# Delta rule: its inputs loaded in front of the cache copies, and the copies made in 4 KB rows, keys and values apart

## What is computed

```python
cache = caches[gi]                       # (8, min(win, 1024), 2, 8, 128): rows of keys and values
L = cache.shape[1]
kv_new = jnp.stack([k[:, :, gi], v[:, :, gi]], axis=2)
kv_all = jnp.concatenate([cache, kv_new], axis=1)
keep = min(win, L + T)                   # T = 4
bufs.append(kv_all[:, L + T - keep:])    # returned as the new cache
```

```python
vnew = ui - wi @ S
o = (qi * exp(gi)) @ S + ai @ vnew
S = S * exp(glast) + (ki * exp(glast - gi)).T @ vnew
```

## Time and profile before

| what | value |
|---|---|
| median of 3 runs | 2547.58 us (2545.9 to 2551.32) |
| the profiled execution | 2549.36 us, of it 2547.6 us in the span |
| TensorE busy | 2061.0 us, 81% of the span |
| VectorE busy | 1281.7 us, 50% |
| ScalarE busy | 778.5 us, 31% |
| GpSimd busy | 645.0 us, 25% |
| DMA | 874.97 MB moved, mean 343 GB/s |
| norm phase | 8.6 to 21.2 us |
| input projection | 21.2 to 117.7 us |
| convolution phase | 117.7 to 239.1 us |
| delta phase | 239.1 to 462.2 us |

### The profile page before, as it was taken

One profiled execution on the slowest core, in us unless ns is written; L12 is line 12 of the kernel. 1 busy time (PEld: TensorE's weight loads), 2 busy tenths in 40 slices (PEclk: granted clock), 3 DMA queues, 4 the chain that ended last, 5 costly groups with the idle time before them and its releaser, 6 DMA issues. The chain is left out here.

```text
span 2547.6 us, 25620 instructions
## 1 busy us (share of the span) xinstructions
PE 2061.0 (81%) x9026; PEld 1031.3 (40%) x9026; DVE 1281.7 (50%) x3157; ACT 778.5 (31%) x2275; POOL 645.0 (25%) x645
## 2 busy tenths in 40 slices
PE   7893797478787898877699999987888887988766
PEld 5682685243222243322244464554532222432222
DVE  0084643264677667775511031123556677666754
ACT  1141100024444344443411122121234444344443
POOL 0000000034443444434201000000344434454341
PEclk9985766789999999998799999999899999999978
DMA  5894999679999999999938755753899999999995
GB/s 196 306 339 137 335 331 332 236 268 405 427 427 427 427 427 414 427 426 427 411 147 335 276 200 206 284 199 125 338 426 426 427 427 427 426 423 427 427 427 243
DMA packets 129427, 874.97 MB, mean 343 GB/s; under 512 B 15876, under 2 KB 29700, under 8 KB 45195
## 3 DMA queue, kind: packets, MB, share of 16 engines
q0 software_dynamic: 92160, 662.74, 62.6%
q1 hardware_dynamic: 37139, 210.60, 23.4%
HBM read 861.98 MB, written 118.81 MB: 385 GB/s over the span
## 5 line engine op out<-in xcount | busy, mean ns | idle before, releaser
L1430 PE MATMUL tail_acc<-tail_ring,tail_diag 128*128 128x512 f32 x1216 | 597.7, 622 | 111.5 <-ACT tail_diag L1289 110.6
L1177 DVE CUSTOM_DVE_ANT_0 tail_ring<-tail_ring,all_h 128x1024 f32<-128x1024 f32 x344 | 418.8, 1223 | 235.8 <-DMA tail_ring<-in_peer_uv,tail_idx 235.3
L1430 PE MATMUL tail_acc<-mid_wring,tail_diag 128*128 128x512 f32 x832 | 413.3, 624 | 98.7 <-ACT tail_diag L1289 98.5
L1570 POOL DMA_INDIRECT mid_wring<-in_peer_uv,tail_idx x232 | 239.0, 1030 | 1001.7 <-DVE all_x L1062 525.8
L1570 POOL DMA_INDIRECT tail_ring<-in_peer_uv,tail_idx x344 | 369.4, 1074 | 480.4 <-PE tail_acc L1430 410.8
L1430 PEld LDWEIGHTS tail_acc<-tail_ring,tail_diag 128*128 128x128 f32 x1216 | 217.0, 193 | 477.2 <-ACT tail_diag L1289 297.3
L1177 DVE CUSTOM_DVE_ANT_0 mid_wring<-mid_wring,all_h 128x1024 f32<-128x1024 f32 x232 | 283.3, 1223 | 175.4 <-DMA mid_wring<-in_peer_uv,tail_idx 174.1
L1283 ACT ACTIVATE tail_gelus<-tail_dots 128x1 f32<-128x1 f32 x576 | 116.2, 202 | 723.3 <-DVE tail_dots L1177 723.0
L1430 PEld LDWEIGHTS tail_acc<-mid_wring,tail_diag 128*128 128x128 f32 x832 | 147.8, 193 | 352.6 <-ACT tail_diag L1289 223.9
L1681 PE MATMUL mix_acc<-mid_wring,all_hT 128*128 128x512 f32 x576 | 273.4, 610 | 1.5 <-PEq L80 1.4
L1289 ACT ACTIVATE tail_diag<-all_ident,tail_weights 128x128 f32<-128x128 f32 x512 | 205.5, 401 | 26.4 <-PE tail_acc L1430 9.9
(11 more groups left out here) (363 smaller groups left out, 2099.3 us busy)
## 6 DMA issues: line engine op xcount, KB each, us to landing
mid_wring<-in_w_qkv SPq DMA_DIRECT2D x18, 2048.0 KB, 8.8
out_kv_s<-in_cache_kv_w SPq DMA_DIRECT2D x8, 4064.0 KB, 49.2
mix_ring<-in_kT POOLq DMA_DIRECT2D x16, 1024.0 KB, 8.1
mix_ring<-in_v_rows POOLq DMA_DIRECT2D x16, 1024.0 KB, 10.3
ab_ring_w<-in_w_in_ab SPq DMA_DIRECT2D x6, 2048.0 KB, 11.4
mix_ring<-in_kT POOLq DMA_DIRECT2D x16, 768.0 KB, 9.3
mix_ring<-in_v_rows POOLq DMA_DIRECT2D x16, 768.0 KB, 9.0
mid_wring<-in_w_out SPq DMA_DIRECT2D x4, 2048.0 KB, 10.4
```

The costliest lines, as they stand in the source:

```text
L1177: V.tensor_tensor_reduce(out=u, in0=u, in1=h[:, g, :], scale=1.0, scalar=0.0, op0=ALU.mult, op1=ALU.add, accum_out=dots[:, n:n + 1]).then_ ...
L1430: last = mm(acc[g][:, c * 512:(c + 1) * 512], diag[:, n % DIAGS, :], v[:, c * 512:(c + 1) * 512], start=first, stop=final)
L1570: pool.indirect_dma_start(slot(r), None, table, bass.IndirectOffsetOnAxis(ap=idx[:, j, i:i + 1], axis=0)).then_inc(landed[r], 16)
```

## The change

The allocation of the delta phase's loaded tiles and the list of their 14 loads move into a new function, `delta_inputs`, called in front of the norm phase; the tiles live from there to the end of the delta phase. `first_norm_phase` gets the list as `later` and SP issues it right behind the three chunks of weights. `delta_phase` takes the tiles and the semaphore. In `roll_cache` every copy becomes two, one of the keys and one of the values, each of `keep` rows of 1024 words (4 KB) that lie 8 KB apart on both sides; the last wait counts twice as many.

```diff
--- before.py
+++ after.py
@@ -147,7 +147,7 @@
 
 
-def first_norm_phase(nc, K, T, hT, ahead):
+def first_norm_phase(nc, K, T, hT, ahead, later):
 
     x, xs, h, hs = K["x"], K["xs"], K["h"], K["hs"]
     with ExitStack() as ctx:
@@ -166,6 +166,8 @@
                 sp.dma_start(gain[:], broadcast_rows(T["norm_mix"][0:1, :], D)).then_inc(gain_in, 16)
                 sp.dma_start(gain_s[:], T["gain_s"][0]).then_inc(gain_in, 16)
                 for to, frm, landed in ahead:
+                    sp.dma_start(to, frm).then_inc(landed, 16)
+                for to, frm, landed in later:
                     sp.dma_start(to, frm).then_inc(landed, 16)
 
             @block.vector
@@ -566,7 +568,22 @@
 
 
-def delta_phase(nc, name, K, T, hT, zT, conv, mixT, cache_out):
+def delta_inputs(P, T):
+
+    G = {"cst": P.sb("masks", [128, 12, 128]), "own": P.sb("owner", [128, DEC_B]), "wab": P.sb("w_ab", [128, KC, 8]),
+         "alog": P.sb("a_log", [128, 4]), "dtb": P.sb("dt_bias", [128, 4]), "gn": P.sb("norm_gain", [128, 1]),
+         "S0": P.sb("S_sample", [128, DEC_B, 4, 128])}
+    loaded = P.sem("delta_loaded")
+    loads = [(G["wab"][:], T["w_in_ab"][0].rearrange("(k p) n -> p k n", p=128)[:, :, IN_AB - 8:IN_AB], loaded),
+             (G["cst"][:], T["c_gdn"].rearrange("p (k n) -> p k n", k=12), loaded),
+             (G["own"][:], T["c_owner"], loaded), (G["alog"][:], broadcast_rows(T["a_log"], 4), loaded),
+             (G["dtb"][:], broadcast_rows(T["dt_bias"], 4), loaded),
+             (G["gn"][:], T["gdn_norm_g"].rearrange("a n -> n a"), loaded)]
+    loads += [(G["S0"][:, b, :, :], T["state_delta"][0, b].rearrange("h k v -> k h v"), loaded) for b in range(DEC_B)]
+    return G, loaded, loads
+
+
+def delta_phase(nc, name, K, T, G, loaded, hT, zT, conv, mixT, cache_out):
 
 
@@ -601,10 +618,7 @@
 
     with ExitStack() as ctx:
         P = Phase(nc, ctx, name)
-        cst = P.sb("masks", [128, 12, 128])
-        own = P.sb("owner", [128, DEC_B])
-        wab = P.sb("w_ab", [128, KC, 8])
-        alog, dtb, gn = P.sb("a_log", [128, 4]), P.sb("dt_bias", [128, 4]), P.sb("norm_gain", [128, 1])
+        cst, own, wab, alog, dtb, gn, S0 = (G[k] for k in ("cst", "own", "wab", "alog", "dtb", "gn", "S0"))
         ab, gt = P.sb("ab", [128, 3, 8]), P.sb("g_tmp", [128, 3, 4])
         beta, g = P.sb("beta", [128, 3, 4]), P.sb("g", [128, 3, 4])
         per_tile = lambda name, shape: [P.sb(f"{name}{t}", shape) for t in range(3)]
@@ -618,12 +632,11 @@
         Rv, Rk, kd = per_tile("Rv", [128, 4, 128]), per_tile("Rk", [128, 4, 128]), P.sb("k_decay", [128, 3, 4, 128])
         u, wT, qe = P.sb("u", [128, 3, 4, 128]), P.sb("wT", [128, 3, 4, 128]), P.sb("q_exp", [128, 3, 4, 128])
         S, vn, vs = P.sb("S", [128, 4, 128]), P.sb("v_new", [128, 4, 128]), P.sb("v_new_s", [NS, 4, 128])
-        S0 = P.sb("S_sample", [128, DEC_B, 4, 128])
         wS, vm = P.sb("wS", [128, 4, 32]), P.sb("v_owner", [32, DEC_B, 128])
         oT, ones = P.sb("oT", [128, 4, NTOK]), P.sb("ones", [128, 128])
         sqr = P.sb("sqr", [128, 4, NTOK])
         bank = [P.ps(f"bank{i}", [128, 512]) for i in range(8)]
-        loaded, dve_steps, act_steps, stored = (P.sem(s) for s in ("loaded", "dve_steps", "act_steps", "stored"))
+        dve_steps, act_steps, stored = (P.sem(s) for s in ("dve_steps", "act_steps", "stored"))
         turn = {"gates": P.sem("gate_turn"), "main": P.sem("main_turn")}
         turn.update({t: P.sem(f"tile{t}_turn") for t in range(3)})
         heads = [b[:].rearrange("q (h c) -> q h c", h=4) for b in bank]
@@ -654,16 +667,6 @@
         with nc.Block() as block:
             @block.sync
             def _(sp):
-                sp.dma_start(wab[:], T["w_in_ab"][0].rearrange("(k p) n -> p k n", p=128)[:, :, IN_AB - 8:IN_AB]
-                             ).then_inc(loaded, 16)
-                sp.dma_start(cst[:], T["c_gdn"].rearrange("p (k n) -> p k n", k=12)).then_inc(loaded, 16)
-                sp.dma_start(own[:], T["c_owner"]).then_inc(loaded, 16)
-                sp.dma_start(alog[:], broadcast_rows(T["a_log"], 4)).then_inc(loaded, 16)
-                sp.dma_start(dtb[:], broadcast_rows(T["dt_bias"], 4)).then_inc(loaded, 16)
-                sp.dma_start(gn[:], T["gdn_norm_g"].rearrange("a n -> n a")).then_inc(loaded, 16)
-                for b in range(DEC_B):
-                    sp.dma_start(S0[:, b, :, :], T["state_delta"][0, b].rearrange("h k v -> k h v")
-                                 ).then_inc(loaded, 16)
                 roll_cache(sp, T, 2, cache_out)
                 sp.wait_ge(turn["main"], at["main", "c3 S dve"] + 1)
                 sp.dma_start(T["out_delta_p"][0, 0].rearrange("h k v -> k h v"), S[:]).then_inc(stored, 16)
@@ -2244,17 +2247,18 @@
 
         with ExitStack() as c2:
             P0 = Phase(nc, c2, "l0")
+            G, delta_loaded, delta_loads = delta_inputs(P0, T)
             zT, conv = P0.sb("zT", [128, 24, NTOK]), P0.sb("conv", [128, 12, NTOK])
             with ExitStack() as c3:
                 W = WeightRing(Phase(nc, c3, "ab_ring"), T["w_in_ab"][0], IN_AB - 8, 3)
-                first_norm_phase(nc, K, T, hT, W.start)
+                first_norm_phase(nc, K, T, hT, W.start, delta_loads)
                 def copies(sp):
                     roll_cache(sp, T, 0, cache_out)
                     roll_cache(sp, T, 1, cache_out, range(2))
 
                 columns_phase(nc, "ab", hT, T["w_in_ab"][0], IN_AB - 8, zT, ahead=W, after=copies)
             conv_phase(nc, "cv", K, T, zT, mixT, conv, cache_out)
-            delta_phase(nc, "gd", K, T, hT, zT, conv, mixT, cache_out)
+            delta_phase(nc, "gd", K, T, G, delta_loaded, hT, zT, conv, mixT, cache_out)
 
         with ExitStack() as c2:
             P1 = Phase(nc, c2, "mid")
@@ -2266,7 +2270,7 @@
         with nc.Block() as block:
             @block.sync
             def _(sp):
-                sp.wait_ge(cache_out, 16 * NG * DEC_B)
+                sp.wait_ge(cache_out, 16 * 2 * NG * DEC_B)
 
 def roll_cache(eng, T, gi, cache_out, samples=range(DEC_B)):
@@ -2275,8 +2279,9 @@
     keep = dst.shape[1] - DEC_T
     drop = src.shape[1] - keep
     for b in samples:
-        eng.dma_start(dst[b, 0:keep].rearrange("r k h e -> r (k h e)"),
-                      src[b, drop:].rearrange("r k h e -> r (k h e)")).then_inc(cache_out, 16)
+        for kv in range(2):
+            eng.dma_start(dst[b, 0:keep, kv].rearrange("r h e -> r (h e)"),
+                          src[b, drop:, kv].rearrange("r h e -> r (h e)")).then_inc(cache_out, 16)
 
 HOST_LAID = ("peer_u", "peer_v", "w_in_c", "w_out_ab", "w_out_c", "ple_gate", "peer_wq", "ple_proj", "peer_keys", "p_prompt",
```

## The result

The changed kernel takes **2813.8 us** (median of 4 runs, 2812.15 to 2815.86), the one before 2546.74 us (4 runs): a ratio of 1.1047, 95% interval 1.103 to 1.1064. It is 267 us slower; the forecast was 2790, with a range of 2770 to 2885. The profiled execution has a span of 2811.7 us.

A forecast was written before the change was run, and what follows sets the result against it. TensorE's 32.7 us wait for `S_sample` before the delta rule was the target, with a DMA bound 2.5 us behind compute. The profiled 2549.4 + 256 - 13.5 = 2791.9, less 1.8 for the median, gave 2790 us, range 2770 to 2885.

The forecast's parts named there:

- part 3: Group 0 and 1 copies: 124 and 508 rows run on four engines, 396 us; convolution phase ends at 495 us, +256.
- part 1: Norm phase: SP issues the 14 moved loads behind 6 MB of weights, delaying the projection by +15 us.
- Part 2: Delta phase: TensorE starts with the phase, which is bound by DMA at 209.6 us against 223.1, -13.5 us.
- my 26.4 and 39.8: Norm phase: when SP ends its loads, with an empty queue (26.4 us) or all waiting for the weights (39.8).
- two bounds: Group 0 and 1 copies: all 16 engines, or the largest count up to 16 giving equal shares, four; four taken.
- my 128 an engine: Projection phase: the queue takes about 128 rows an engine, so SP leaves at 227 us with about 128 left.
- about 252: Convolution phase: TensorE starts at about 252 us, its loads standing behind 128 rows (20 us).
- the 223 us that I had named as a sign of being wrong: Delta phase: a length above 223 us would show the forecast wrong; 210 us with share 1.00 would show it right.
- 7.3 us behind the copies: Delta phase: state stores land 7.3 us after group 2's copies, taken from copies ending near 454 and stores in at 461.3.
- the copies were not spread evenly: Rival for group 0 and 1 copies: rows dealt over all 16 engines, copies stay hidden, 2549 us; chance 0.04.
- nothing came out faster: Rival: 16 engines and the norm phase growing by only 5.9 us, so -7.6 us, 2540 us; chance 0.03.
- not twice that: Rival for copies on four engines: a 4 KB row costs twice 156 ns, copies take 790 us, near 3185; chance 0.03.

The follow-up runs named there:

- the kernel with 112 + 12 rows: Against the changed kernel, each copy of 124 or 508 rows became two DMAs, 112 + 12 or 496 + 12 rows: 2579.82 us, ratio 1.0112.

## Why the prediction was right, and where a term was off

It was right in its main mechanism, part 3, and in part 1. Part 2 came out the other way than forecast.

- **Part 1** (+15 us): right. The projection starts 14.0 us later. The full queue held SP as said: 4.85 and 5.00 us for the loads of `w_ab` and the masks, done only at 34.3 us, between my 26.4 and 39.8. Shown to be SP's arrival alone: with the loads behind the barrier the 14 us are gone.
- **Part 3** (four engines, convolution phase to 495 us): right, in the engines (share 0.26), in the rate (106 GB/s for 105) and in the end (495.6). The step on which it all rests, the largest divisor up to 16, was a choice between two bounds; it is now shown at 4, 8, 13 and 16. SP left the projection phase at 216 and not 228 us, so the queue took in more rows than my 128 an engine. That changed nothing, as said: its next two loads stood 20.1 us in the issue, and the first matmul came at 252.84. The "about 252" has some luck in it: 228 + 20 is 248, and the other 4 us have no term.
- **Part 2** (delta phase 209.6 us, a gain of 13.5): its first half was right, TensorE starts 0.05 us after the phase. The phase was bound by DMA, as said, but the size of that bound was wrong by 19 us: it lasted 228.9, a loss of 5.8, and passed the 223 us that I had named as a sign of being wrong. Two terms were mis-sized. The rate was taken as 334 GB/s for any row; 4 KB rows moved at 317, so 67.1 MB take 212 us and not 201. That each engine could move 26 GB/s by itself did not show that sixteen together would keep their rate; why they lose 5% stays open. And the stores were given 7.3 us behind the copies. The copies ended near 495.7 + 212 = 708, the stores 3.8 us after their last issue at 719.6, at 723.4: 15.7 us. Compute was done at 699.0, so that all of this showed. SP now sits in the issue of the copies until 690.0 and is held another 12.0 us by the first store, and from 704 us on the queue no longer fills the engines:

```profile
697.65 1.36 DVE L931 TENSOR_TENSOR all_mixT<-gd_oT,l_zT 128x1152 f32<-128x1152 f32 x1
...
704.00:718.00 14.00, 0.50 0.63 221
```

That the late issues cause the idle engines is argued from these rows and was not tested. In the kernel with 112 + 12 rows the same sum gives 261.3 + 67.1 / 0.310 = 478 and an end at 493.6, again about 16.
- **Behind the delta phase**: 2087.2 us for 2085.4, nothing of weight.
- **The sum.** The forecast for the span was +242.5; it was +264.1, of which 19.3 are the delta phase, 1.8 the rest and 0.5 the convolution phase. The time is near 2790 for the reason that was given: the convolution phase ends 256.5 us later (256 forecast). Part 2 is small beside that, and so its wrong sign does little to the sum. The rivals fell: the copies were not spread evenly, nothing came out faster, and four engines took some 400 us (about 91 to 490) for their 2528 rows each, 158 ns a row for the 156 taken, and not twice that.

## What to carry to other kernels

In these copies from DRAM to DRAM the shape in which a DMA is written decides how many DMA engines carry it: give it an outermost count divisible by 16, and cut a remainder off into a small DMA of its own. Where the copies are hidden behind other work, 13 engines did as well as 16, and 4 cost 257 us. A DMA whose rows no longer join into one stretch loses the equal cutting that it had; look at the shape that the program ends up with, and at the DMA share in the windows. And a load moved ahead is only free where the engine that issues it has time and the queue has room: the same 14 loads cost 5 us in one phase and gave 11 in the next, and then the phase that they had held was bound by the copies, which had to move too.

## What I had not expected of the hardware

- On 16 engines, copies from DRAM to DRAM lose 5% when 64 KB pieces become 8 KB rows (334 to 317 GB/s on one chip) or 4 KB rows, keys and values apart (328 to 310 on another), at a DMA share of 0.99 or 1.00, although an engine alone has time to spare: four engines moved 25.5 GB/s each in 4 KB rows, sixteen only 19.4 (310 / 16). The share thus says how many engines are occupied, and not how fast they are.
- The idle engines take nothing over in hundreds of microseconds: from 110 to 480 us the share was 0.26, four engines of 16, while SP was blocked in its issues by the queues of these four.
